# The two pool products of a hybrid decoder layer: from fp32 matmuls to split float32r passes, two slots later

## The reference, cut to what matters

```python
h = rms_norm(x, norm_mix_pre[l])
proj = jnp.einsum('bsd,de->bse', h, w_in[l])
u_pool, g_b, g_c, u_conv, q, k, v = jnp.split(proj, offsets, axis=-1)
y_pool = pool_mixer(u_pool, pool_w[l], pool_scale[l])   # d = trailing mean - token, then a 64x64 map per group
y_conv = g_b * causal_dwconv(g_c * u_conv, conv_w[l])
y_attn = swa_sink_attention(q, k, v, attn_sinks[l])
mix = jnp.einsum('bse,ed->bsd', jnp.concatenate([y_pool, y_conv, y_attn], axis=-1), w_o[l])
x = x + rms_norm(mix, norm_mix_post[l])
```

## Time and profile before

| what | us |
|---|---|
| median of 3 runs (949.88 to 950.55) | 950.21 |
| span of the profiled execution, first to last instruction | 948.2 |
| PE busy in that span | 938.9 |
| DVE busy | 654.7 |
| ACT busy | 433.5 |
| POOL busy | 189.4 |

### The profile page before, as it was taken

How to read it: one execution, slowest core, us unless ns; L and a number is a source line. 1 busy time by engine, 2 the same in 40 slices (tenths; PEclk the granted TensorE clock), 3 DMA queues, 4 the chain that set the end, 5 groups by cost and what they waited for, 6 DMA issues and landing times.

```text
span 948.2 us, 11487 instructions
## 1 busy us (share of the span) xinstructions
PE 938.9 (99%) x4419; PEld 777.9 (82%) x4419; DVE 654.7 (69%) x710; ACT 433.5 (46%) x648; POOL 189.4 (20%) x182
## 2 busy tenths in 40 slices
PE   8999999999999999999999999999999999999997
PEld 7988887887888888888888888888888888888886
DVE  6645795766655899777877787778776653535668
ACT  5524444444433555445443444444444454335353
POOL 3301000000111424242223333443431100000021
PEclk9999999999999999999999999999999999999999
DMA  6999971005322236486343446554647775677455
GB/s 225 269 328 231 209 145 45 23 23 178 134 89 89 90 97 206 142 184 183 115 141 100 145 112 133 112 143 105 140 91 208 201 235 214 228 267 264 163 171 200
DMA packets 114248, 151.16 MB, mean 159 GB/s; under 512 B 6289, under 2 KB 66193, under 8 KB 114193
## 3 DMA queue, kind: packets, MB, share of 16 engines
q1 hardware_dynamic: 100737, 118.63, 38.5%
q0 software_dynamic: 13456, 31.79, 16.8%
HBM read 113.17 MB, written 60.29 MB: 183 GB/s over the span
## 4 chain that ended last, share of the span: by engine, by line
PE 97%; DVE 1%; DMA 0%; ACT 0%; POOL 0%; issue 0%; DVEq 0%; POOLq 0%; SPq 0%; ACTq 0%
PE ps L1616 30%; PE ps L1618 30%; PE ps L1617 30%; PE ps L1626 1%; PE ps L1751 1%; PE ps L1774 1%; PE ps L1752 1%; PE ps L1760 1%; PE ps L1778 1%; DMA xin<-in_x 0%; DVE hlo L1138 0%; PE ps L1789 0%; DVE ps L1155 0%; PE ps L1664 0%; DVE x2b L1427 0%
## 5 line engine op out<-in xcount | busy, mean ns | idle before, releaser
L1616 PE MATMUL ps<-hhi,whi 128*128 128x512 f32 (+1 forms) x240 | 91.1, 379 | 0.5 <-DVE hlo L1138 0.5
L1618 PE MATMUL ps<-hhi,wlo 128*128 128x512 f32 (+1 forms) x240 | 88.5, 369 | 0.0
L1617 PE MATMUL ps<-hlo,whi 128*128 128x512 f32 (+1 forms) x240 | 88.5, 369 | 0.0
L686 POOL TENSOR_TENSOR w_sums<-wraw 128x1024 f32<-128x1024 f32 x20 | 48.4, 2421 | 185.8 <-DVE w2lo L1373 63.0
L648 POOL TENSOR_SCALAR meansq<-sumsq 128x1 f32<-128x1 f32 x28 | 10.0, 357 | 373.4 <-ACT yg L1042 170.8
L1616 PEld LDWEIGHTS ps<-hhi,whi 128*128 128x128 f32 x240 | 45.3, 189 | 8.0 <-DVE hlo L1138 0.7
L1001 ACT ACTIVATE yg<-ps,par_b 128x1024 f32<-128x1024 f32 x21 | 25.3, 1207 | 57.9 <-DVE ps L1499 57.9
L1618 PEld LDWEIGHTS ps<-hhi,wlo 128*128 128x128 f32 x240 | 45.2, 189 | 7.7
L1617 PEld LDWEIGHTS ps<-hlo,whi 128*128 128x128 f32 x240 | 45.3, 189 | 7.4 <-issue 0.5
L1447 DVE SCALAR_TENSOR_TENSOR yg<-ps,par_a,yg 128x1023 f32<-128x1023 f32 x22 | 28.2, 1282 | 26.9 <-ACT yg L1001 26.9
L1616 PE MATMUL ps<-h2hi,whi 128*128 128x512 f32 x116 | 45.4, 391 | 0.2 <-DVE wraw L1148 0.2
(11 more groups left out here) (261 smaller groups left out, 2709.1 us busy)
## 6 DMA issues: line engine op xcount, KB each, us to landing
wraw<-in_ffn_w_up SPq DMA_DIRECT2D x42, 512.0 KB, 5.2
s_dram<-in_ffn_w_down POOLq DMA_DIRECT2D x6, 2816.0 KB, 28.1
wraw<-r_dram SPq DMA_DIRECT2D x44, 256.0 KB, 3.7
wraw<-s_dram SPq DMA_DIRECT2D x44, 256.0 KB, 4.9
r_dram<-cst SPq DMA_DIRECT2D x33, 256.0 KB, 2.8
wraw<-act_dram SPq DMA_DIRECT2D x33, 256.0 KB, 3.6
wraw<-in_ffn_w_down SPq DMA_DIRECT2D x33, 256.0 KB, 4.6
wraw<-in_w_in SPq DMA_DIRECT2D x14, 512.0 KB, 10.2
```

What stands on the lines that cost most here:

```text
L686: pool.tensor_tensor(w_sums[:, 0:2, :], raw[:, 0:4:3, :], raw[:, 2:3, :].broadcast_to([P, 2, HALF]), ALU.add)\
L1616: pe.matmul(acc, w_hi, x_hi, start=first, stop=False, skip_group_check=looped)
L1617: pe.matmul(acc, w_hi, x_lo, start=False, stop=False, skip_group_check=looped)
L1618: return pe.matmul(acc, w_lo, x_hi, start=False, stop=last, skip_group_check=looped)
```

## The change

- The pool products move from slots 8 and 10 to slots 10 and 12, with their PSUM copies on ACT (`copy_pooled`), which follow the same constant.
- `pool_product` uses the split operands and `product`: 6 float32r matmuls of 512 columns in place of 2 fp32 ones (4 records).
- ACT gets three rounding copies: the two matrices after unit 6's exponentials (128x256), d of product 0 at the end of unit 8 (128x1024, behind the gate's evacuation, waiting for `pool_ready` 2), and d of product 1 at the end of unit 10 (waiting for product 0, since `pool_hi` is one buffer).
- DVE gets three subtractions: the matrices at the head of unit 7's mixer work, d of product 0 in unit 9's mixer work, d of product 1 in unit 11's mixer work ahead of the conv taps. Unit 9's norming moves ahead of its mixer work, which was empty before.
- `pool_hi` lies where `pool_u` was; the low parts lie in place over `pool_d` and `pool_mat`; the rounded matrices get room of their own. No DMA is added, removed or moved.

```diff
-POOL_SLOT = (8, 10)
+POOL_SLOT = (10, 12)
...
+            def round_pool_mat():
+                act.wait_ge(pool_w_in, 64)
+                act.activation(pool_mat_hi[:, :, :], pool_mat[:, :, :], ACT.Copy)\
+                   .then_inc(pool_mat_rounded, 1)
+
+            def round_pool(i):
+                if i == 0:
+                    act.wait_ge(pool_ready, 2)
+                else:
+                    act.wait_ge(pool_mixed, 1)
+                act.activation(pool_hi[:, :], pool_d[:, i, :], ACT.Copy).then_inc(pool_rounded, 1)
...
                 exps(u)
                 if u in POOL_SLOT:
                     copy_pooled(POOL_SLOT.index(u))
+                if u == 6:
+                    round_pool_mat()
                 if u == 8:
                     evacuate(2)
+                    round_pool(0)
+                if u == POOL_SLOT[0]:
+                    round_pool(1)
...
+            def low_pool_mat():
+                dve.wait_ge(pool_mat_rounded, 1)
+                dve.tensor_tensor(pool_mat_lo[:, :, :], pool_mat[:, :, :], pool_mat_hi[:, :, :],
+                                  ALU.subtract).then_inc(pool_mat_split, 1)
+
+            def low_pool(i):
+                dve.wait_ge(pool_rounded, i + 1)
+                dve.tensor_tensor(pool_lo[:, i, :], pool_d[:, i, :], pool_hi[:, :], ALU.subtract)\
+                   .then_inc(pool_split, 1)
...
+                if u == 7:
+                    low_pool_mat()
                 if u == 8:
                     pool_means(1)
+                if u == 9:
+                    low_pool(0)
+                if u == 11:
+                    low_pool(1)
...
-                if 4 <= u < 9 or u == 11:
+                if 4 <= u < 10 or u == 11:
                     norm_probs(u)
                 mixer_work(u)
-                if u in (0, 1, 3) or u >= 9 and u != 11:
+                if u in (0, 1, 3) or u >= 10 and u != 11:
                     norm_probs(u)
...
             def pool_product(i):
-                if i == 0:
-                    pe.wait_ge(pool_w_in, 64)
-                pe.wait_ge(pool_ready, i + 1)
+                pe.wait_ge(pool_mat_split, 1)
+                pe.wait_ge(pool_split, i + 1)
                 pe.wait_ge(s_masked, POOL_SLOT[i] + 1)
                 for c in range(2):
-                    last = pe.matmul(ps[:, 4 + c, :], pool_mat[:, i, :],
-                                     pool_d[:, i, c * HALF:(c + 1) * HALF],
-                                     start=True, stop=True)
+                    cols = slice(c * HALF, (c + 1) * HALF)
+                    last = product(ps[:, 4 + c, :], pool_mat_hi[:, i, :], pool_mat_lo[:, i, :],
+                                   pool_hi[:, cols], pool_lo[:, i, cols], True, True)
                 last.then_inc(pool_mixed, 1)
```

More of the change, by code:

```diff
@@ L174, in build @@
         par_rows = alloc(xb_, "par_rows", [P, 2, P])
+        pool_mat_hi = alloc(xb_, "pool_mat_hi", [P, 2, P], F32R)
         xb_.close()
@@ L180, in build @@
         xb2.close()
+        xb3 = ExitStack()
+        alloc(xb3, "under_pool_hi", [P, 3 * SEQ])
+        pool_hi = alloc(xb3, "pool_hi", [P, SEQ], F32R)
+        alloc(xb3, "under_pool_lo", [P, 2 * SEQ + 3 * PAD])
+        pool_lo = alloc(xb3, "pool_lo", [P, 2, SEQ], F32R)
+        alloc(xb3, "under_pool_mat_lo", [P, NT, P])
+        pool_mat_lo = alloc(xb3, "pool_mat_lo", [P, 2, P], F32R)
+        xb3.close()
         xc = ExitStack()
@@ L319, in build @@
         pool_ready = sem("pool_d_ready")
+        pool_mat_rounded = sem("pool_weights_rounded")
+        pool_mat_split = sem("pool_weights_split")
+        pool_rounded = sem("pool_d_rounded")
+        pool_split = sem("pool_d_split")
         pool_mixed = sem("pool_product_done")
```

## The result

The changed kernel takes 951.80 us (median of 18 runs, 951.43 to 952.53) against 950.26 for the kernel before on the same chips (18 runs, 949.88 to 950.57): 1.54 us more, a ratio of 1.0017 with a 95% interval of 1.001 to 1.0023. Forecast were 951.5 and +1.27.

What follows compares the result with a forecast made beforehand. PE's work was taken to bound the kernel (97% of the span). Products -0.68, slot 10's wait +1.88 and slot 12's +0.07 gave +1.27 us on 950.21: 951.5, range 949.4 to 952.6.

Steps and rivals of the forecast that it cites:

- The products: Slots 10 and 12: each product takes 1.38 us instead of 1.72, both together -0.68 us.
- The wait in slot 10: PE waits 1.88 us before the transposes of unit 9's probabilities, which are ready later while PE is due earlier.
- matrices: DVE, head of unit 7's mixer work: subtraction for the matrices' low part delays unit 9's chain by 0.33 us.
- rounding: ACT, end of unit 8: rounding d of product 0 delays unit 9's probabilities by 0.95 us.
- The hand-over from DVE to PE: Slot 10: PE starts the transposes 0.09 us after the DVE instruction it waited for.
- the budget: Skill page's estimate for ACT's rounding copy: 1.15 us, making slot 10's wait 2.08; the forecast kept the row's 0.95.
- The second wait: Slot 12: product 1 waits 0.07 us for unit 12's masking, behind DVE's subtraction; rival of a large wait, 952.5, chance 0.10.
- The norming's price: DVE, unit 9: leaving the norming behind the new subtraction would have added another 1.13 us to slot 10's wait.
- The clock: Rival: PE's clock falls in slot 10's wait and coming back costs 1.8 us, giving 953.3; chance 0.03.
- a margin of 1.21: Slot 10 before the change: unit 9's normed probabilities end 1.21 us before the transposes that wait for them start.

Runs made afterwards that it cites:

- The saving alone shows in the last two runs: Repaired order of PE with unsplit fp32 products, 950.25 us, and the changed kernel with waits removed by reordering, 949.64, beside the kernel before at 950.23.
- the move alone: Kernel before with its fp32 products moved to slots 10 and 12 and nothing split: 951.0 us against 950.41, ratio 1.0006.
- the upper group of that run's times: Changed kernel with unit 9's norming put back behind product 0's subtraction: median 952.93 us against 950.35; three of six times at 953.70 to 953.78.

## Why the prediction was right, and where it wasn't

It was right in kind and nearly in size: +1.27 forecast, +1.54 measured, inside the range and within 0.2%; the stage itself costs 1.42 in the trace. (Over 18 runs of each kernel the interval leaves out 1 all the same.)

- *The products.* Forecast 1.38 each, measured 1.39 in slot 10; slot 12's took 1.48 (175.88 to 177.36) with the slow step described below. The saving alone shows in the last two runs: 0.61 for 0.68.
- *The wait in slot 10.* Forecast 1.88. The transposes start at 155.28 where 154.46 - 1.72 + 0.72 = 153.46 was due: 1.82. Its terms hold one by one: matrices 0.34 for 0.33 (moved away: 0.3 of wait less), rounding 0.95 for 0.95 (moved: 0.9 less; doubled: 1.1 more), the move alone 0.6 for 0.6. The hand-over from DVE to PE was 0.06 (155.22 to 155.28) for 0.09. For the rounding the row was right and the budget was not the one for this copy: the Trainium skill ("ScalarE: Activation LUTs", section "Rules for kernel authors") gives the 0.3 us for an activation whose bias is a pointer operand, and this copy is given no bias. The trace shows the 0.95 of the row.
- *The second wait.* Forecast 0.07, measured 0.12.
- *What was left out.* After a wait the first steps are slower: the transposes take 0.41 to the next matmul (155.28 to 155.69) where 0.36 was usual (slot 12: 172.57 to 172.92 was 0.35), and product 1's first step 0.31 for 0.23. That is 0.13. With it the stage adds up: -0.65 for the products without that slow step, 1.82, 0.12 and 0.13 give the 1.42 of the trace. The 0.12 from there to the 1.54 of the medians is below what the runs resolve.
- *The norming's price.* "Another 1.13 would have come on top" failed: it is 0.5, since DVE idled 0.60 ahead of the norming, waiting for the exponentials. That idle time was in the trace of before as well, ahead of the norming's first step in unit 9; I priced the instruction and forgot the gap it would fill. The forecast didn't use this price.

```profile
152.15 0.16 DVE L1251 TENSOR_TENSOR small<-small 128x4 f32<-128x4 f32 x1 [0.61 <-ACT small L828]
```

- *The clock.* The rival's price came near (1.8 forecast, 1.5 measured when it happened), though by a row that doesn't show it: over the warm-up matmuls (1.26 to 7.00) the granted clock of the trace reads 1.00. For this kernel the rival lost, but the argument against it was wrong, so that part was luck. I read from the end of the trace that the clock outlasts 4.4 us of idle; with the rounding doubled it fell behind a wait of 2.78, after PE had already resumed. The changed kernel stands at most 1.1 us of waiting away from a further 1.5 us.

## What to carry to other kernels

When an engine without idle time loses a piece of work, everything behind it is due earlier, and the results that others make for it, where they don't hang on its work behind that place, are not; before moving work away from a place, look up the margin of each result that is waited for behind that place. Here a margin of 1.21 met 1.72 from one side and 1.25 from the other, and a gain of 0.7 became a loss of 1.5. Work on engines that are half idle is free only off the chain that ends in such a wait: the same copy behind the score copy cost PE no wait (0.77 is left, which the move alone, 0.42, and the matrices' step, 0.34, account for), and filling the bound engine's wait with work that was at hand anyway (the transposes behind twelve matmuls, then the product behind the rest) gave the gain back.

## What the runs showed of the hardware that was not expected

The granted clock can fall after the idle time is over: with a wait of 2.78 us it read 1.00 during the wait and 0.50 (1.2 GHz) in the work behind it, from 157.07 on where that work began at 155.88, at a price of 1.5 us. With waits of 1.68 and 2.15 it read 1.00 throughout; each of these is one profiled execution. The Trainium skill's page on TensorE's clock gate ("TensorE: Matmul & The Clock Gate", section "Part 1: The HAM clock gate") has the default clock as the slow one that activity lifts; this run agrees in direction, with the fall behind 2.78 us without work and 1.00 again from 160.6 on, after PE had worked without a break since 155.88. So a wait of TensorE cost half as much again in the work behind it. Whether the fall can also come behind the wait of 2.15, as the upper group of that run's times suggests, no trace here shows.
